# Four quarters of x are turned by VectorE's block transposes and DRAM trips instead of TensorE transposes

## The chip, the cores and the metric

The kernel runs on one core of one Trainium2 chip, in one launch. The metric is the device time of an execution in microseconds (us). Three runs of the kernel before took 2202.17, 2202.65 and 2204.27 us; their median is 2202.65 us.

## The reference

Two transformer-like blocks on a sequence of 256 tokens of width 2048, all in float32. The first block, cut to what matters here:

```python
mem_n = rms_norm(mem, norm_mem_g)
h = rms_norm(x, norm_in_g)                       # x: (1, 256, 2048)
proj = h @ w_in                                  # to qa ka va za qb kb vb zb qm zm gates
mk, mv = split(mem_n @ w_mem_kv)
...                                              # three attentions, gated, projected, merged
x = x + merged @ w_out
x = rms_norm(x, norm_final_g)
```

The second block (an RG-LRU, a retention and a gated feed-forward layer) follows on the result. The change touches only the way from x to its transposed operand of `h @ w_in`; the same numbers are to come out.

## The kernel before, in words

**Products.** Every product takes the activations as the stationary operand, with the 2048 (or more) inputs on the partitions, and streams 512 output columns of a weight matrix. To keep float32 precision each operand is split into a high part (`_hi`, fp32r) and a rest (`_lo`), and three matmuls are summed: hi*hi, hi*lo, lo*hi (L1485, L1486, L1487). A tile of 512 output columns is worked off in eight **weight chunks**; a chunk is 256 rows of the weights (512 KB) and costs 12 matmuls (two groups of 128 rows, two groups of 128 tokens, three products). Chunks are numbered through the program in this text: g0 to g31 are the four tiles of `w_mem_kv` (`tiles_memkv`), eight a tile, and g32 is the first chunk of `w_in` (`tiles_attention`), the first that needs x.

**A chunk's way.** SyncE loads it into one of four slots of `raw` (L451); ScalarE makes `w_hi` of it (L575, `split`); VectorE makes `w_lo` (L861, `split`); TensorE multiplies. ScalarE waits for the slot to be free again (`w_used`), VectorE for ScalarE (`hi_ready`), TensorE for VectorE (`lo_ready`), SyncE for VectorE. So the engines in front of TensorE can be at most four chunks ahead of it. The order on each engine is fixed: `run` walks the chunks of a tile, and after the split of chunk h of the tile come that engine's hooks for h (`act_hooks`, `dve_hooks`; `pe_hooks` on TensorE come after the matmuls of a chunk).

**x's operand.** x comes in as token rows (`x_tok`, L467). In the tiles 2 and 3 of `tiles_memkv` TensorE transposes one **quarter** (512 of the 2048 columns) at a time (`job`, L1345: 8 transposes of 128x128 into PSUM, after g18, g20, g26 and g28); ScalarE scales them into `xT_hi` (`job_hi`, L607), VectorE makes `xT_lo` (`job_lo`, L898). ScalarE also takes x's sums of squares (`squares`, L584, after its split of g15), and VectorE makes from them x's factors after its split of g17 (`x_factors`): it sends the mean to GpSimd, which takes a power (`norm_root(1)`, L497), and goes on when that is back (L880).

**The other way to turn.** The results of projections that must be transposed go by another way already, called a **trip** here. VectorE turns 32x32 blocks of `stage` into `tmp` (`turn_blocks`, L1023, `z_made`), GpSimd's queue writes `tmp` to a DRAM scratch (L513), waits until it has landed (`b_out`), and reads it back with four DMAs that put the blocks where they belong (`carry`, L518, `b_in`). ScalarE then copies out of `stage` (`use_late`, L729). GpSimd does the trips one after another, in the order of its program. In `tiles_memkv` there are two, for the two halves of mkT: trip 1 (turned after g11) and trip 2 (turned after VectorE's split of g19, `post`: L1050 and L1023).

## Time and profile before

| | us |
|---|---|
| runs (3), median | 2202.65 |
| lowest, highest | 2202.17, 2204.27 |
| profiled execution, its own time | 2204.24 |
| profiled execution, span | 2202.4 |
| TensorE busy in the span | 2185.7 (99%) |
| VectorE busy | 1308.7 (59%) |
| ScalarE busy | 1025.3 (47%) |

The span is what the trace covers of the profiled execution, from its first to its last event; 1.84 us of that execution's time lie around it. The profiled execution is 1.59 us above the median of the runs. Times inside the trace count from the start of the span.

### The profile page before, as it was taken

How to read it: one execution, taken by the hardware profiler on the slowest of the kernel's cores; microseconds unless marked ns; L12 is line 12 of the kernel's file. 1: busy time of each engine (PE TensorE's matmuls, PEld its weight loads, DVE VectorE, ACT ScalarE, POOL GpSimd, SP SyncE). 2: the span in 40 equal slices, each digit the busy share in tenths (PEclk: the TensorE clock that was granted, in tenths of full speed). 3: DMA queues.
4: the chain of work that ended last, by engine and by line, in shares of the span. 5: the costliest groups of instructions: out<-in, count | busy, mean ns of one | idle time of the engine just before them, and what ended most of it. 6: DMA issues, size and time to landing. Idle time of an engine off the chain costs nothing.

```text
span 2202.4 us, 26200 instructions
## 1 busy us (share of the span) xinstructions
PE 2185.7 (99%) x9906; PEld 1811.4 (82%) x9906; DVE 1308.7 (59%) x1646; ACT 1025.3 (47%) x1235; POOL 144.2 (7%) x242
## 2 busy tenths in 40 slices
PE   9999999999999999999999999999999999999998
PEld 7888888887888888888888888888888888888886
DVE  5655656666455645546676878665555555554454
ACT  5544444443444444444554666454444444444443
POOL 0010101011000000000111100110001000100000
PEclk9999999999999999999999999999999999999999
DMA  8775656567754657667778756586777777776664
GB/s 293 219 230 177 203 164 214 182 225 220 219 163 148 211 177 229 201 204 282 228 259 249 229 182 200 192 247 210 211 211 225 220 211 211 227 236 193 194 194 146
DMA packets 228673, 464.65 MB, mean 211 GB/s; under 512 B 16344, under 2 KB 16608, under 8 KB 227680
## 3 DMA queue, kind: packets, MB, share of 16 engines
q1 hardware_dynamic: 212128, 408.73, 59.9%
q0 software_dynamic: 15712, 53.49, 8.0%
q8 instruction: 63, 1.03, 0.2%
q10 hardware_dynamic: 736, 1.12, 0.1%
q14 instruction: 34, 0.28, 0.0%
HBM read 437.59 MB, written 25.69 MB: 210 GB/s over the span
## 4 chain that ended last, share of the span: by engine, by line
PE 90%; DVE 4%; DMA 3%; ACT 1%; issue 1%; POOL 0%; POOLq 0%; ACTq 0%; DVEq 0%
PE ps L1485 29%; PE ps L1487 29%; PE ps L1486 29%; DVE w_lo L861 1%; DMA stage<-bounce 1%; PE ps L1345 1%; ACT w_hi L575 1%; PE ps L1376 1%; PE ps L1398 1%; DMA bounce<-tmp 1%; DVE tmp L1023 1%; DVE tmp L1014 0%; DVE stage L1009 0%; DVE stage L1018 0%; DMA raw<-in_w_out 0%
## 5 line engine op out<-in xcount | busy, mean ns | idle before, releaser
L861 DVE TENSOR_TENSOR w_lo<-raw,w_hi 128x1024 fp32r<-128x1024 f32 (+1 forms) x776 | 931.5, 1211 | 766.8 <-ACT w_hi L575 764.9
L575 ACT ACTIVATE w_hi<-raw 128x1024 fp32r<-128x1024 f32 (+1 forms) x776 | 810.3, 1050 | 917.2 <-PE ps L1487 824.5
L1485 PE MATMUL ps<-w_hi,xT_hi 128*128 128x512 f32 x1088 | 430.2, 395 | 1.6 <-DVE w_lo L861 1.6
L1487 PE MATMUL ps<-w_hi,xT_lo 128*128 128x512 f32 x1088 | 424.2, 390 | 0.0
L1486 PE MATMUL ps<-w_lo,xT_hi 128*128 128x512 f32 x1088 | 423.6, 389 | 0.0
L1485 PE MATMUL ps<-w_hi,u2T_hi 128*128 128x512 f32 x704 | 274.0, 389 | 0.0
L1487 PE MATMUL ps<-w_hi,u2T_lo 128*128 128x512 f32 x704 | 273.9, 389 | 0.0
L1486 PE MATMUL ps<-w_lo,u2T_hi 128*128 128x512 f32 x704 | 273.9, 389 | 0.0
L1485 PEld LDWEIGHTS ps<-w_hi,xT_hi 128*128 128x128 f32 x1088 | 204.4, 188 | 44.1 <-DVE w_lo L861 3.3
L1487 PEld LDWEIGHTS ps<-w_hi,xT_lo 128*128 128x128 f32 x1088 | 204.2, 188 | 43.5
L1486 PEld LDWEIGHTS ps<-w_lo,xT_hi 128*128 128x128 f32 x1088 | 204.5, 188 | 40.7
L1486 PEld LDWEIGHTS ps<-w_lo,u2T_hi 128*128 128x128 f32 x704 | 132.2, 188 | 27.5
L1487 PEld LDWEIGHTS ps<-w_hi,u2T_lo 128*128 128x128 f32 x704 | 132.2, 188 | 27.3
L1485 PEld LDWEIGHTS ps<-w_hi,u2T_hi 128*128 128x128 f32 x704 | 132.2, 188 | 27.3
L1485 PE MATMUL ps<-w_hi,uT_hi 128*128 128x512 f32 x384 | 152.3, 397 | 0.0
L1487 PE MATMUL ps<-w_hi,uT_lo 128*128 128x512 f32 x384 | 149.7, 390 | 0.0
L1486 PE MATMUL ps<-w_lo,uT_hi 128*128 128x512 f32 x384 | 149.5, 389 | 0.0
L1485 PE MATMUL ps<-w_hi,ffT_hi 128*128 128x512 f32 x336 | 130.7, 389 | 0.0
L1486 PE MATMUL ps<-w_lo,ffT_hi 128*128 128x512 f32 x336 | 130.7, 389 | 0.0
L1487 PE MATMUL ps<-w_hi,ffT_lo 128*128 128x512 f32 x336 | 130.7, 389 | 0.0
L513 POOL DMA_DIRECT2D bounce<-tmp x41 | 23.9, 583 | 1360.6 <-DVE tmp L1023 1360.6
L518 POOL DMA_DIRECT2D stage<-bounce x164 | 98.8, 631 | 142.7 <-DMA bounce<-tmp 137.1
(262 smaller groups left out, 2259.3 us busy)
## 6 DMA issues: line engine op xcount, KB each, us to landing
raw<-in_w_in SPq DMA_DIRECT2D x368, 512.0 KB, 4.5
raw<-in_w_ffn_gate SPq DMA_DIRECT2D x88, 512.0 KB, 4.3
raw<-in_w_ffn_up SPq DMA_DIRECT2D x88, 512.0 KB, 4.5
raw<-in_w_ffn_down SPq DMA_DIRECT2D x88, 512.0 KB, 4.0
raw<-in_w_out SPq DMA_DIRECT2D x64, 512.0 KB, 5.1
bounce<-tmp POOLq DMA_DIRECT2D x41, 512.0 KB, 3.3
...
```

The costliest lines, as they stand in the source:

```text
L513: pool.dma_start(bounce, tmp[:, :, :].rearrange("p t n -> p (t n)")).then_inc(b_out, 16)
L518: pool.dma_start(stage[32 * m:32 * (m + 1), :, :].rearrange("p t (q x) -> p t q x", q=4), bounce.rearrange("(q a) (t m x) -> m a t q x", a ...
L575: nc.scalar.activation(w_hi[:, s, 0:per], raw[:, s, 0:per], ACT.Copy).then_inc(hi_ready, 1)
L861: nc.vector.tensor_tensor(w_lo[:, s, 0:per], raw[:, s, 0:per], w_hi[:, s, 0:per].bitcast(F32), ALU.subtract)\
L1023: ins = nc.vector.transpose(tmp[:, t], src(t).rearrange("p (c m a) -> p m c a", c=4, m=4))
L1345: ins = nc.tensor.transpose(ps[:, o:o + P], src(t, c), ident)
L1376: ins = nc.tensor.matmul(ps[:, o:o + P], qT[:, qc, t * P:(t + 1) * P], kT[:, kc, kt * P:(kt + 1) * P], start=n == 0, stop=n == len(qs) - 1)
L1398: ins = nc.tensor.matmul(ps[:, o:o + width], probsT[:, a + n * P:a + (n + 1) * P], v(kt), start=n == 0, stop=n == len(blocks) - 1)
L1485: nc.tensor.matmul(bank(2 * par + t), x_hi, w_hi[:, s, k], start=first, stop=False)
L1486: nc.tensor.matmul(bank(2 * par + t), x_hi, w_lo[:, s, k], start=False, stop=False)
L1487: ins = nc.tensor.matmul(bank(2 * par + t), x_lo, w_hi[:, s, k], start=False, stop=last)
```

## The change

TensorE's four jobs on x are gone, and with them `job_hi` and `job_lo` for x. For each quarter q of x now:

- VectorE transposes the quarter's 32x32 blocks from `x_tok` into `x_tmp[q % 2]` (`x_turn(q)`, two instructions), after its splits of g15, g19, g23 and g27;
- GpSimd's queue takes it through a DRAM scratch of its own into `x_stage[q % 2]` (`carry_x(q)`: one DMA out, a wait until it has landed, four DMAs in);
- ScalarE makes `xT_hi` from `x_stage` (`x_hi(q)`, four instructions), after its splits of g20, g24, g28 and g32;
- VectorE makes `xT_lo` (`x_lo(q)`, four instructions), after its splits of g21, g25, g29 and g33.

TensorE waits for `xT_lo`'s quarters before g32, g34, g36 and g38. The loads of x come in another order (both token halves of a quarter one after the other, the same eight DMAs), with a semaphore for each quarter.

```diff
...
         zm = at("zm", [P, NT, 1024], F32, 144)
         mv = at("mv", [P, NT, 1024], F32, 152)
         mkT = at("mkT", [P, 8, S], F32, 160)
+        x_tmp, x_stage = ([at(f"{n}{k}", [P, NT, NW], F32, kib + 4 * k) for k in range(2)] for n, kib in (("x_tmp", 168), ("x_stage", 176)))
         half_at = (120, 160)
         qaT, kaT, va, za = (
             [at(f"{n}{h}", s, F32, half_at[h] + 4 * m) for h in range(2)]
...
         ls8 = small[:, 118:126]
         lam = cols[:, V_LAM:V_LAM + 8]
         bounce = nc.dram_tensor("bounce", (P, NT * NW), F32, kind="Internal").ap()
-        turned = stage[:, :, :].rearrange("p t (q c b) -> p c (t q) b", c=QUAD, b=32)
+        x_bounce = [nc.dram_tensor(f"x_bounce{k}", (P, NT * NW), F32, kind="Internal").ap() for k in range(2)]
+        turned, *x_quarter = (m[:, :, :].rearrange("p t (q c b) -> p c (t q) b", c=QUAD, b=32) for m in (stage, *x_stage))
 
         def by_block(ap):
             return ap.rearrange("p c (u b) -> p c u b", b=32)
...
         dve_link = sem("dve_link")
         in_mem = [sem(f"in_mem{q}") for q in range(QUAD)]
         in_tables = sem("in_tables")
-        in_x = [sem("in_x0"), sem("in_x1")]
+        in_x = [sem(f"in_x{q}") for q in range(QUAD)]
         in_const, in_vec, in_res, in_g1, in_dec, in_gw, in_g2 = (
             sem(n) for n in ("in_const", "in_vec", "in_res", "in_g1", "in_dec", "in_gw", "in_g2"))
         spilled, in_h2, stored = sem("spilled"), sem("in_h2"), sem("stored")
         x_added, row_made = sem("x_added"), sem("row_made")
+        x_turned, x_out, x_hi_made, x_lo_made = (sem(n) for n in ("x_turned", "x_out", "x_hi_made", "x_lo_made"))
+        x_in = [sem(f"x_in{q}") for q in range(QUAD)]
         t0_done, t0_hi, t0_lo = (sem(n) for n in ("t0_done", "t0_hi", "t0_lo"))
         acc_done, rows_added, rows_sq, rows_mean, rows_root, rows_scaled = (
             sem(n) for n in ("acc_done", "rows_added", "rows_sq", "rows_mean", "rows_root", "rows_scaled"))
...
 
             def load_x(t, q):
                 c = slice(q * NW, (q + 1) * NW)
-                sp.dma_start(x_tok[:, t, c], x[t * P:(t + 1) * P, c]).then_inc(in_x[t], 16)
+                sp.dma_start(x_tok[:, t, c], x[t * P:(t + 1) * P, c]).then_inc(in_x[q], 16)
 
             sp.dma_start(ident, consts_d[:, C_ID:C_ID + P]).then_inc(in_const, 16)
             load_mem(0)
             first, second, *rest = tiles_memkv()
             load(first, {0: lambda: load_mem(1), 2: lambda: load_mem(2), 3: lambda: load_mem(3)})
-            load(second, {h: lambda h=h: load_x(h // QUAD, h % QUAD) for h in range(NT * QUAD)})
+            load(second, {h: lambda h=h: load_x(h % NT, h // NT) for h in range(NT * QUAD)})
             sp.dma_start(consts[:, C_ID + P:], consts_d[:, C_ID + P:]).then_inc(in_tables, 16)
             load_all(rest + tiles_attention() + tiles_merge(0))
             w.rounds(sp, NG - 1, lambda i: load_all(tiles_merge(i + 1)))
...
                         pool.dma_start(stage[32 * m:32 * (m + 1), :, :].rearrange("p t (q x) -> p t q x", q=4),
                                        bounce.rearrange("(q a) (t m x) -> m a t q x", a=32, t=NT, m=4)[m]).then_inc(b_in, 16)
 
+            def carry_x(q):
+                pool.wait_ge(x_turned, q + 1)
+                pool.dma_start(x_bounce[q % 2], x_tmp[q % 2][:, :, :].rearrange("p t n -> p (t n)")).then_inc(x_out, 16)
+                pool.wait_ge(x_out, 16 * (q + 1))
+                for m in range(4):
+                    pool.dma_start(x_stage[q % 2][32 * m:32 * (m + 1), :, :].rearrange("p t (q x) -> p t q x", q=4),
+                                   x_bounce[q % 2].rearrange("(q a) (t m x) -> m a t q x", a=32, t=NT, m=4)[m]).then_inc(x_in[q], 16)
+
             norm_root(0, R["mem"]["r"])
             carry(1, 1)
+            carry_x(0)
             norm_root(1, R["x"]["r"])
-            carry(2, 17)
+            carry(2, 2)
+            for q in range(1, QUAD):
+                carry_x(q)
+            carry(3, 17)
             pool.wait_ge(w_used, G_X + SLOTS)
             for t in range(NT):
                 pool.dma_start(x1[:, t], x[t * P:(t + 1) * P, :]).then_inc(in_res, 16)
...
             four[0]["act_hooks"] = {1: jobs(memT_hi, V_MEM, 1), 3: jobs(memT_hi, V_MEM, 2), 5: jobs(memT_hi, V_MEM, 3),
                                     6: [mem_in, lambda: squares(mem_tok, sumsq_m, lambda t: None)]}
             four[1]["act_hooks"] = {7: [lambda: act.wait_ge(b_out, 16),
-                                        lambda: squares(x_tok, sumsq_x, lambda t: act.wait_ge(in_x[t], 16 * QUAD))]}
-            for n in (2, 3):
-                four[n]["act_hooks"] = {6: jobs(xT_hi, V_IN, 2 * n - 4), 7: jobs(xT_hi, V_IN, 2 * n - 3)}
-            last = four[3]["act_hooks"].pop(7)
-            four[3]["act_hooks"][5] = [log_sigmoid_exp]
+                                        lambda: squares(x_tok, sumsq_x, lambda t: [act.wait_ge(s, 16 * NT) for s in in_x])]}
+            def x_hi(q):
+                act.wait_ge(x_in[q], 64)
+                for c in range(QUAD):
+                    kc = q * QUAD + c
+                    ins = nc.scalar.activation(xT_hi[:, kc].rearrange("p (u b) -> p u b", b=32), x_quarter[q % 2][:, c], ACT.Copy,
+                                               scale=cols[:, V_IN + kc:V_IN + kc + 1])
+                ins.then_inc(x_hi_made, 1)
+
+            four[2]["act_hooks"] = {4: [lambda: x_hi(0)]}
+            four[3]["act_hooks"] = {0: [lambda: x_hi(1)], 4: [lambda: x_hi(2)], 5: [log_sigmoid_exp]}
             act.dma_start(vec_a[:, :], vecs[0:P]).then_inc(in_vec, 16)
             act.dma_start(vec_b[0:V_END - P, :], vecs[P:V_END]).then_inc(in_vec, 16)
             act.wait_ge(pool_c, 1)
...
             four[0]["act_hooks"][0] = [second_half]
             prev = chain(four, None)
             tiles = tiles_attention()
-            tiles[0]["act_hooks"] = {1: last}
+            tiles[0]["act_hooks"] = {0: [lambda: x_hi(3)]}
             prev = chain(tiles, prev)
             prev = chain(tiles_merge(0, first=True), prev)
             w.rounds(act, NG - 1, lambda i: chain(tiles_merge(i + 1), merge_last(i)))
...
 
             four[0]["dve_hooks"] = {0: [second_half], 1: jobs(memT_hi, memT_lo, V_MEM, 1), 3: jobs(memT_hi, memT_lo, V_MEM, 2),
                                     5: jobs(memT_hi, memT_lo, V_MEM, 3), 7: [mem_factors]}
-            for n in (2, 3):
-                four[n]["dve_hooks"] = {6: jobs(xT_hi, xT_lo, V_IN, 2 * n - 4), 7: jobs(xT_hi, xT_lo, V_IN, 2 * n - 3)}
-            last = four[3]["dve_hooks"].pop(7)
-            four[2]["dve_hooks"][1] = [x_factors]
+            def x_turn(q):
+                dve.wait_ge(in_x[q], 16 * NT)
+                if q >= 2:
+                    dve.wait_ge(x_out, 16 * (q - 1))
+                for t in range(NT):
+                    ins = nc.vector.transpose(x_tmp[q % 2][:, t], x_tok[:, t, q * NW:(q + 1) * NW].rearrange("p (c m a) -> p m c a", c=4, m=4))
+                ins.then_inc(x_turned, 1)
+
+            def x_lo(q):
+                dve.wait_ge(x_hi_made, q + 1)
+                for c in range(QUAD):
+                    kc = q * QUAD + c
+                    lo, hi = (m.rearrange("p (u b) -> p u b", b=32) for m in (xT_lo[:, kc], xT_hi[:, kc].bitcast(F32)))
+                    ins = nc.vector.scalar_tensor_tensor(lo, x_quarter[q % 2][:, c], cols[:, V_IN + kc:V_IN + kc + 1], hi,
+                                                         ALU.mult, ALU.subtract)
+                ins.then_inc(x_lo_made, 1)
+
+            four[1].setdefault("dve_hooks", {})[7] = [lambda: x_turn(0)]
+            four[2]["dve_hooks"] = {1: [x_factors], 3: [lambda: x_turn(1)], 5: [lambda: x_lo(0)], 7: [lambda: x_turn(2)]}
+            four[3]["dve_hooks"] = {1: [lambda: x_lo(1)], 3: [lambda: x_turn(3)], 5: [lambda: x_lo(2)]}
             first_lo(t0_hi, range(2), t0_lo)
             prev = chain(four, None)
             log_sigmoid()
             tiles = tiles_attention()
-            tiles[0]["dve_hooks"] = {1: last}
+            tiles[0]["dve_hooks"] = {1: [lambda: x_lo(3)]}
             prev = chain(tiles, prev)
             prev = chain(tiles_merge(0, first=True), prev)
             w.rounds(dve, NG - 1, lambda i: chain(tiles_merge(i + 1), merge_last(i)))
...
             four = tiles_memkv()
             begin(four[0], mem_tok, in_mem)
             four[0]["need"][0].append(lambda: pe.wait_ge(cols_ready, 1))
-            for n in (2, 3):
-                four[n]["pe_hooks"] = {k: [lambda q=q: job(q, x_tok, in_x)] for k, q in ((2, 2 * (n - 2)), (4, 2 * (n - 2) + 1))}
             prev = chain(four, None)
             tiles = tiles_attention()
-            tiles[0]["need"] = {0: [lambda: pe.wait_ge(tx_free[0], w.n["j0"] - 1), lambda: pe.wait_ge(tx_free[1], w.n["j1"] - 1)],
-                                4: [lambda: pe.wait_ge(tx_free[0], w.n["j0"])],
-                                6: [lambda: pe.wait_ge(tx_free[1], w.n["j1"])]}
+            tiles[0]["need"] = {2 * q: [lambda q=q: pe.wait_ge(x_lo_made, q + 1)] for q in range(QUAD)}
             prev = chain(tiles, prev)
             tiles = tiles_merge(0, first=True)
             for k, units in ((3, 4), (4, 12), (5, 16)):
```

In the names below, `x_tmp_64`, `x_tmp_65` and `x_stage_66`, `x_stage_67` are the two buffers of each kind. The line numbers after the change are 4 to 34 higher.

GpSimd's queue from trip 1 of mkT on, before: `bounce` and `stage` are mkT's trips, the TENSOR_TENSOR is the power for x's factors.

```order
L497 TENSOR_TENSOR small<-small,mneg_c 128x2
L513 DMA bounce<-tmp 128x1024
L518 DMA stage<-bounce 32x8x128 x4
L497 TENSOR_TENSOR small<-small,mneg_c 128x2
L513 DMA bounce<-tmp 128x1024
L518 DMA stage<-bounce 32x8x128 x4
```

The same place after the change:

```order
L517 DMA bounce<-tmp 128x1024
L522 DMA stage<-bounce 32x8x128 x4
L527 DMA x_bounce<-x_tmp_64 128x1024
L530 DMA x_stage_66<-x_bounce 32x8x128 x4
L501 TENSOR_TENSOR small<-small,mneg_c 128x2
L517 DMA bounce<-tmp 128x1024
L522 DMA stage<-bounce 32x8x128 x4
L527 DMA x_bounce<-x_tmp_65 128x1024
L530 DMA x_stage_67<-x_bounce 32x8x128 x4
L527 DMA x_bounce<-x_tmp_64 128x1024
L530 DMA x_stage_66<-x_bounce 32x8x128 x4
```

The trip of x's quarter 0 now stands between trip 1 of mkT and the power; those of the quarters 1 to 3 stand behind trip 2 of mkT (the last of them is cut off here).

ScalarE from x's squares on, before (the first row of splits is g16 to g19, and so on):

```order
L584 ACTIVATE sq_out,small<-x_tok 128x2048 x2
L575 ACTIVATE w_hi<-raw 128x1024 x4
L729 ACTIVATE mkT<-stage 128x1024
L575 ACTIVATE w_hi<-raw 128x1024 x3
L607 ACTIVATE xT_hi<-ps,cols 128x256 x4
L575 ACTIVATE w_hi<-raw 128x1024
L607 ACTIVATE xT_hi<-ps,cols 128x256 x4
L575 ACTIVATE w_hi<-raw 128x1024 x4
```

The same place after the change:

```order
L600 ACTIVATE sq_out,small<-x_tok 128x2048 x2
L591 ACTIVATE w_hi<-raw 128x1024 x4
L745 ACTIVATE mkT<-stage 128x1024
L591 ACTIVATE w_hi<-raw 128x1024
L805 ACTIVATE xT_hi<-x_stage_66,cols 128x256 x4
L591 ACTIVATE w_hi<-raw 128x1024 x4
L805 ACTIVATE xT_hi<-x_stage_67,cols 128x256 x4
L591 ACTIVATE w_hi<-raw 128x1024 x3
```

ScalarE now makes `xT_hi` of quarter 1 between its splits of g24 and g25, out of `x_stage_67`.

VectorE from its split of g16 on, after the change (the row ahead of them is quarter 0's block transposes):

```order
L1306 STREAM_TRANSPOSE x_tmp_64<-x_tok 128x512 x2
L883 TENSOR_TENSOR w_lo<-raw,w_hi 128x1024 x2
L890 TENSOR_SCALAR small<-small 128x2
L902 TENSOR_TENSOR small<-small 128x2
...
L883 TENSOR_TENSOR w_lo<-raw,w_hi 128x1024 x2
L1072 TENSOR_SCALAR stage<-ps,small 128x512 x2
L1045 STREAM_TRANSPOSE tmp<-stage 128x512 x2
L1306 STREAM_TRANSPOSE x_tmp_65<-x_tok 128x512 x2
L883 TENSOR_TENSOR w_lo<-raw,w_hi 128x1024 x2
L1314 SCALAR_TENSOR_TENSOR xT_lo<-x_stage_66,cols,xT_hi 128x256 x4
```

Two pairs of block transposes of x are new here, one ahead of the factors' wait for GpSimd (L902) and one behind the turning of mkT's second half.

## Rows read from the trace of the kernel before

**Rows 1.** The page of the profile: busy times, and the chain that ended last.

```profile
PE 2185.7 (99%) x9906; PEld 1811.4 (82%) x9906; DVE 1308.7 (59%) x1646; ACT 1025.3 (47%) x1235; POOL 144.2 (7%) x242
...
PE 90%; DVE 4%; DMA 3%; ACT 1%; issue 1%; POOL 0%; POOLq 0%; ACTq 0%; DVEq 0%
```

**Rows 2.** The timeline of TensorE (start us, us, what): g18, first job, g24, g25.

```profile
62.17 0.39 PE L1485 MATMUL ps<-w_hi,memT_hi 128*128 128x512 f32 x1
...
64.66 0.39 PE L1487 MATMUL ps<-w_hi,memT_lo 128*128 128x512 f32 x1
64.89 1.03 PE L1345 MATMUL ps<-consts,x_tok 128*128 128x128 f32 x8
65.69 0.48 PE L1485 MATMUL ps<-w_hi,memT_hi 128*128 128x512 f32 x1
66.00 0.40 PE L1486 MATMUL ps<-w_lo,memT_hi 128*128 128x512 f32 x1
...
80.31 0.39 PE L1485 MATMUL ps<-w_hi,memT_hi 128*128 128x512 f32 x1
...
83.03 0.39 PE L1485 MATMUL ps<-w_hi,memT_hi 128*128 128x512 f32 x1
```

**Rows 3.** The instructions of line L1345 (duration min/median/max in ns), first 160 us.

```profile
L1345 PE MATMUL ps<-consts,x_tok x32: 270/272/273, 64.9 to 95.6; 128*128 128x128 f32 x32
```

**Rows 4.** The timeline of VectorE, g15 to g20; brackets give the idle time before.

```profile
49.47 1.23 DVE L861 TENSOR_TENSOR w_lo<-raw,w_hi 128x1024 fp32r<-128x1024 f32 x1 [1.95 <-ACT w_hi L575]
...
57.12 0.16 DVE L868 TENSOR_SCALAR small<-small 128x2 f32<-128x2 f32 x1
58.12 0.16 DVE L880 TENSOR_TENSOR small<-small 128x2 f32<-128x2 f32 x1 [0.84 <-POOL small L497]
...
59.60 1.22 DVE L861 TENSOR_TENSOR w_lo<-raw,w_hi 128x1024 fp32r<-128x1024 f32 x1 [0.40 <-ACT w_hi L575]
...
62.54 1.40 DVE L1050 TENSOR_SCALAR stage<-ps,small 128x512 f32<-128x512 f32 x2
63.98 1.30 DVE L1023 STREAM_TRANSPOSE tmp<-stage 128x512 f32<-128x512 f32 x2
```

**Rows 5.** The timeline of ScalarE, its split of g24.

```profile
73.74 1.08 ACT L575 ACTIVATE w_hi<-raw 128x1024 fp32r<-128x1024 f32 x1
```

**Rows 6.** The timeline of GpSimd: trips 1 and 2, the power between, a later trip.

```profile
41.21 0.75 POOL L513 DMA_DIRECT2D bounce<-tmp  x1 [8.26 <-DVE tmp L1023]
49.51 2.42 POOL L518 DMA_DIRECT2D stage<-bounce  x4 [7.56 <-DMA bounce<-tmp]
57.37 0.72 POOL L497 TENSOR_TENSOR small<-small,mneg_c 128x2 f32<-128x2 f32 x1 [5.43 <-DVE small L868]
65.58 0.62 POOL L513 DMA_DIRECT2D bounce<-tmp  x1 [7.49 <-DVE tmp L1023]
70.39 2.41 POOL L518 DMA_DIRECT2D stage<-bounce  x4 [4.19 <-DMA bounce<-tmp]
...
152.94 0.57 POOL L513 DMA_DIRECT2D bounce<-tmp  x1 [14.70 <-DVE tmp L1023]
156.46 2.41 POOL L518 DMA_DIRECT2D stage<-bounce  x4 [2.94 <-DMA bounce<-tmp]
```

**Rows 7.** The stretch 49 to 60 us: busy times, granted clock, DMA share, GB/s.

```profile
49.00:60.00 11.00, 11.00 (x50) 9.10 (x49) 5.20 (x11) 7.40 (x8) 3.14 (x5) 1.00 1.01 304
```

**Rows 8.** The line L518, 0 to 300 us: issue to landing of its 24 DMAs.

```profile
DMA to landing us min/median/max: 3.7/4.6/8.2
```

**Rows 9.** The timeline of ScalarE, stretch 1058 to 1064: four copies out of stage.

```profile
1059.81 1.69 ACT L721 ACTIVATE uT_hi<-stage,cols 128x256 fp32r<-128x256 f32 x4
```

**Rows 10.** The chain in order of time at the start (start us, us, what).

```profile
3.30 0.44 PE ps L1563
...
9.37 0.43 PE ps L1539
...
10.35 0.23 PE ps L1538
```

## Prediction

> **What bounds the kernel now.** I read the page first: TensorE is busy for 99% of the span, and the chain that ended last is 90% TensorE [rows 1]. So only two things move the end: time that TensorE no longer spends, and time that it newly stands still. VectorE (59%) and ScalarE (47%) have room on average, but they run at most four chunks ahead of TensorE, so a wait of some 10 us on either reaches it. Next I read TensorE's timeline around the jobs on x. A chunk takes 2.72 us (g24 to g25 is 83.03 - 80.31) [rows 2]. Last, the timelines of VectorE, ScalarE and GpSimd between 40 and 75 us, where the change puts its pieces. The reader should see there how small the lead is: VectorE has g18 ready at 60.82 (59.60 + 1.22) [rows 4], TensorE starts it at 62.17 [rows 2].
>
> **What is removed.** Four jobs of 8 transposes on TensorE. A single transpose is recorded as 272 ns [rows 3], but they overlap, so I take the price from the starts around a job. From the matmul at 64.66 to the second one after the job, at 66.00, are 1.34 us; without the job it would be two spacings of 0.227 (2.72 / 12), so a job costs 0.89 us [rows 2]. Four jobs: 3.55 us, all of it on the path. Two lie ahead of g25, two behind. ScalarE's and VectorE's 16 + 16 copies out of PSUM are replaced by as many out of SBUF, which cost about the same (four of ScalarE's out of stage: 1.69 us [rows 9]); that edit is nothing in itself.
>
> The Trainium skill (VectorE: DVE Perf Modes, "The three transpose paths" and "Rules for kernel authors") speaks against the change: for 128x128 it says to use TensorE where a PSUM destination will do, and puts such a transpose at 390 ns. An estimate by that page's figure would put the 16 transposes behind g25 at 6.2 us and the sum below at +1.3 instead of +5.7 us; the spacing that this trace shows is 0.11 us each, and it decides.
>
> **What is added.** Eight block transposes on VectorE (0.65 us each by the pair at 63.98 [rows 4], 5.2 us together) and four DRAM trips, which GpSimd does one after the other with the trips that it has. VectorE's share is small; the trips are not. One trip is, by GpSimd's rows [rows 6]: from the issue of the write to the issue of the first read 8.30 us (41.21 to 49.51), 4.81 (65.58 to 70.39) or 3.52 (152.94 to 156.46), as the DMAs are loaded; 2.42 us for the four reads; then the landing of the last, issued 1.8 us after the first, 3.7 to 8.2 us after its issue, median 4.6 [rows 8].
>
> *Quarter 0's trip and the power.* VectorE's two transposes stand behind g15, which ends at 50.70, in idle time before g16: free, ended at 52.0. GpSimd has just issued trip 1's reads (49.51 + 2.42). It writes quarter 0 at 52.2. The DMAs are full from 49 to 60 us (share 1.01) [rows 7], so I take 6.9 us, between 8.30 and 4.81 and nearer the trip issued in the same crowd: reads from 59.1 to 61.5. Only then comes the power for x's factors, which ran at 57.37 before; it is done at 62.3 instead of 58.1. VectorE stands at L880 (58.12 before [rows 4]) and g18's split is queued behind it. From L880 to g18's split 1.1 us are needed, so g18 is ready at 64.7: TensorE starts it 2.6 us late. g19 is ready at 65.9 (its split is 1.22 too); then mkT's second half is turned (2.7 us, as 62.54 to 65.28), ended at 68.6, and quarter 1's blocks (1.3 us), and g20's split ends at 71.1. TensorE would want g20 at 70.2: another 0.9.
>
> *Quarter 1's trip.* Now GpSimd's queue sets the time. It issues mkT's trip 2 at 68.9 (0.3 after the turn, as before), its reads start at 73.7 (+4.81) and are issued by 76.1 (+2.42). Only now does it write quarter 1; with TensorE's suppliers stalled and the DMAs lighter I take 3.9 (between 3.52 and 4.81): reads from 80.0, the last at 81.8, landed at 86.4 (+4.6).
>
> *Who waits for it.* ScalarE has split g24 at 74.8 [rows 5], perhaps a little later, and stands at `x_hi(1)`. Queued behind it are the splits of g25 and all that follow. After 86.4: 1.69 for `x_hi(1)`, 1.06 for `w_hi` of g25, 1.23 for `w_lo`, 0.1 for the handoffs: TensorE starts g25 at 90.5 instead of 83.03, 7.5 us late. This does not add to the delays of g18 and g20: those are contained in it, since g24 has long been done. The same sum of TensorE's own work, without two jobs, would have started g25 at 81.26; so it stands for about 5 us after g24 (71.1 + 5 x 2.72 = 84.7 at its end, plus a little).
>
> *The rest.* Quarters 2 and 3 go through an empty queue: written at 82.4 and about 95, landed by 92 and 105. ScalarE asks for them after g28 (93 or 94) and g32 (about 101, with four chunks of lead to lose: g33 is wanted at 112). The lead hides both. VectorE's extra work, the block transposes and the log-sigmoid pieces in that stretch fit in the 2.72 us a chunk leaves beside a 1.23 us split. If the cover is gone the next late piece would be g26, whose split stands behind `x_lo(1)` (1.7 us): it is ready at about 93.2, and wanted at 93.2. Behind g32 nothing changes, and TensorE goes through to the end; two jobs less give back 1.77 us.
>
> **Sum.** +7.5 - 1.77 = +5.7 us. On the profiled execution: 2202.4 + 1.84 + 5.7 = 2209.9. That execution lies 1.59 above the median of the runs, so for the median I forecast 2208.4.
>
> *Bounds.* Low: 4.81 for quarter 0's write, 3.52 for the others, landing 3.7: power done at 60.2, mkT turned at 66.5, quarter 1 landed at 81.8, g25 at 85.9: +1.1, or 2203.8. High: 8.30, 4.81, 4.81 and landing 8.2: turned at 70.0, landed at 92.3, g25 at 96.4: +11.6, or 2214.3. Even if the power came as early as before, GpSimd's two trips in a row keep g25 from being earlier than about 84.7, which already eats the 3.55 saved.
>
> **The rivals.** A measurement of this kernel can tell about 0.2% (4.4 us) from no change.
>
> *B, quick trips, no change to be seen.* The same mechanism with its price at the low end. It decides at one point: if quarter 1 has landed before about 85.1 us, the net loss is under 4.4. For it: nearly empty trips take 3.52 and land in 3.7 to 4.6. Against it: the DMA share in this stretch is high, and the first trip of mkT took 8.30. Time: between +1.1 and +4.4, middle 2205.4.
>
> *C, the stall also costs TensorE its clock.* At the start of the trace, where its first instruction comes at 3.30 us, a matmul of 512 columns at 9.37 takes 0.43 us in the chain and one at 10.35 0.23 [rows 10]; that is the lower level of its clock (1.2 GHz) against the higher (2.4). The granted clock reads 1.00 everywhere in the profile, so that view says neither yes nor no. If it falls back in the 5 us at g25, up to 6.5 us (as from 3.30 to 9.80 at the start) run at half speed, 3.2 us lost: +8.9, 2211.6. The Trainium skill (TensorE: Matmul & The Clock Gate, "The HAM clock gate") says that a long enough idle stretch puts the clock down and that it depends on where the stretch falls; no row here shows it after the start. Late landings give about the same time, and go with this case.
>
> *D, the change does its full good.* All trips hidden: -3.55 us, 2199.1. It asks that quarter 1 has landed by about 77, when mkT's trip alone takes until 72 before quarter 1 is written at all. It is the only way to a faster kernel, and even then by under 0.2%.
>
> **How the numbers follow.** Forecast 0.50 (net between +4.4 and +8), B 0.31, C 0.15, D 0.04. Slower by over 0.2%: forecast and C, 0.65. Within 0.2%: B and nearly all of D, 0.34. Faster: 0.01. The range runs from the low bound and a little below it, for half of D, to above C and short of the high bound: 2203.3 to 2213.0; cases of one sign hold most of the chance.
>
> **What would show it.** Right: TensorE has no instruction on `x_tok`; its longest wait is about 5 us on `w_lo`, between 83 and 91 us; ScalarE's longest wait there is on the DMA `x_stage<-x_bounce`, some 10 us, ended near 86; the power on GpSimd runs near 61.5 and not 57.4; every chunk after g40 starts at the same distance from the end as before. Wrong: no wait of TensorE over 2 us between 75 and 95 (B or D), a power at 57 to 58 (quarter 0's trip does not stand in its way), waits on `xT_lo` before g32 to g38, or matmuls over 0.4 us apart after a wait (C).

## The result, and the profile after

The changed kernel takes 2215.25 us, the median of 6 runs (2212.85 to 2216.62); the kernel before, 6 runs with the three of above among them, takes 2202.41 (2199.7 to 2204.27). The ratio is 1.0056 with a 95% interval of 1.0047 to 1.0066: 12.8 us slower. The direction was forecast; the size was not. It lies 6.9 us above the forecast of 2208.4 and above the range's end of 2213.0.

| | before | after |
|---|---|---|
| profiled execution, its own time | 2204.24 | 2216.62 |
| profiled execution, span | 2202.4 | 2214.5 |
| start of g18 | 62.17 | 67.53 |
| start of g25 | 83.03 | 96.21 |

The page of the profile after: busy times and shares of the chain, as [rows 1].

```profile
PE 2185.8 (99%) x9874; PEld 1810.1 (82%) x9874; DVE 1312.2 (59%) x1654; ACT 1026.4 (46%) x1235; POOL 156.5 (7%) x262
...
PE 90%; DVE 4%; DMA 3%; ACT 1%; issue 1%; POOL 0%; POOLq 0%; SPq 0%; ACTq 0%; DVEq 0%
```

TensorE is as busy as before, though 32 instructions have gone, and the rest of the page hardly differs. What tells is TensorE's timeline between 62 and 97 us (start, duration, what; the idle time before it and what ended it in brackets), as [rows 2].

```profile
67.53 0.80 PE L1523 MATMUL ps<-w_hi,memT_hi 128*128 128x512 f32 x1 [4.48 <-DVE w_lo L883]
68.13 0.63 PE L1524 MATMUL ps<-w_lo,memT_hi 128*128 128x512 f32 x1
...
96.21 0.79 PE L1523 MATMUL ps<-w_hi,memT_hi 128*128 128x512 f32 x1 [7.89 <-DVE w_lo L883]
```

Two holes (stretches in which TensorE does nothing): 4.48 us before g18 and 7.89 before g25, both ended by VectorE's `w_lo`. After each, matmuls start 0.41 to 0.6 us apart where they start 0.23 apart elsewhere. GpSimd's timeline tells why the holes are there, as [rows 6].

```profile
50.23 2.43 POOL L522 DMA_DIRECT2D stage<-bounce  x4 [7.58 <-DMA bounce<-tmp]
52.57 0.64 POOL L527 DMA_DIRECT2D x_bounce<-x_tmp  x1
62.08 2.42 POOL L530 DMA_DIRECT2D x_stage<-x_bounce  x4 [8.87 <-DMA x_bounce<-x_tmp]
64.42 0.82 POOL L501 TENSOR_TENSOR small<-small,mneg_c 128x2 f32<-128x2 f32 x1
71.57 0.62 POOL L517 DMA_DIRECT2D bounce<-tmp  x1 [6.33 <-DVE tmp L1045]
76.00 2.42 POOL L522 DMA_DIRECT2D stage<-bounce  x4 [3.81 <-DMA bounce<-tmp]
78.32 0.65 POOL L527 DMA_DIRECT2D x_bounce<-x_tmp  x1
87.58 2.42 POOL L530 DMA_DIRECT2D x_stage<-x_bounce  x4 [8.62 <-DMA x_bounce<-x_tmp]
89.89 0.65 POOL L527 DMA_DIRECT2D x_bounce<-x_tmp  x1
93.75 2.42 POOL L530 DMA_DIRECT2D x_stage<-x_bounce  x4 [3.21 <-DMA x_bounce<-x_tmp]
```

The reader should take the differences between the starts. Quarter 0's write takes 9.51 us (52.57 to 62.08), and the power for x's factors stands behind it and its reads, at 64.42 instead of 57.37. mkT's trip 2 starts at 71.57 instead of 65.58, and its write takes 4.43. Quarter 1's write then takes 9.26 (78.32 to 87.58), quarter 2's 3.86. VectorE's and ScalarE's timelines show the two waits that come of it.

```profile
65.27 0.16 DVE L902 TENSOR_TENSOR small<-small 128x2 f32<-128x2 f32 x1 [7.73 <-POOL small L501]
...
94.93 1.23 DVE L883 TENSOR_TENSOR w_lo<-raw,w_hi 128x1024 fp32r<-128x1024 f32 x1 [14.05 <-ACT w_hi L591]
```

```profile
78.21 1.06 ACT L591 ACTIVATE w_hi<-raw 128x1024 fp32r<-128x1024 f32 x1 [2.32 <-DMA raw<-in_w_mem_kv]
92.25 1.70 ACT L805 ACTIVATE xT_hi<-x_stage,cols 128x256 fp32r<-128x256 f32 x4 [12.98 <-DMA x_stage<-x_bounce]
```

VectorE stood 7.73 us for the power, ScalarE 12.98 us for quarter 1 of x, with the split of g25 queued behind it; VectorE and then TensorE followed. The stretches of 5 us around the second hole (start:end, length, busy time and count of TensorE, its weight loads, VectorE, ScalarE, GpSimd; then granted clock, DMA share, GB/s):

```profile
90.00:95.00 5.00, 0.00 (x0) 0.00 (x0) 0.07 (x1) 2.75 (x6) 1.79 (x4) 0.61 0.46 162
95.00:100.00 5.00, 3.79 (x9) 3.02 (x10) 5.00 (x8) 5.00 (x7) 1.17 (x2) 0.50 0.78 213
...
105.00:110.00 5.00, 5.00 (x23) 4.14 (x23) 3.41 (x7) 1.68 (x3) 1.97 (x4) 1.00 0.94 333
```

The granted clock reads 0.61 and 0.50 there. 0.50 is 1.2 GHz instead of 2.4, and the 0.43 us between matmuls are the same thing seen from the other side. It is back at 1.00 by 105; the matmuls are 0.23 us apart again from 101.43 on.

**The account of the trace.** g25 starts 13.18 us late (96.21 - 83.03). Its twelve matmuls last until 101.43, 5.22 us instead of 2.72: 2.5 more. The two jobs saved behind g25 give back 1.77. That makes 13.9. At the first matmul of g36 (114.77 before, 128.64 after) the two traces are 13.87 apart. Of these, 0.72 us were there already at g14, ahead of quarter 0's block transposes, which leaves 13.15 for the change. The span as a whole is 12.1 longer; the rest is given back where this one execution of the kernel before stood for 2.4 us on `w_lo` far behind (after 130 us) and the other for 0.2, and the traces of experiments 5 and 6 gain there too. It belongs to that execution, not to the change.

### The profile page after: what moved, and what is told of

Read it like the earlier page. It is cut to its first block, busy times and chain, and to the rows that moved or that the text cites. A ratio compares the mean times of both kernels' runs of the same rounds, so it can differ in the third digit from the quotient of the medians.

```text
span 2214.5 us, 26165 instructions
## 1 busy us (share of the span) xinstructions
PE 2185.8 (99%) x9874; PEld 1810.1 (82%) x9874; DVE 1312.2 (59%) x1654; ACT 1026.4 (46%) x1235; POOL 156.5 (7%) x262
## 3 DMA queue, kind: packets, MB, share of 16 engines
q8 instruction: 63, 1.03, 0.2%
## 4 chain that ended last, share of the span: by engine, by line
PE 90%; DVE 4%; DMA 3%; ACT 1%; issue 1%; POOL 0%; POOLq 0%; SPq 0%; ACTq 0%; DVEq 0%
PE ps L1523 29%; PE ps L1525 29%; PE ps L1524 29%; DVE w_lo L883 1%; ACT w_hi L591 1%; DMA x_bounce<-x_tmp 1%; PE ps L1414 1%; PE ps L1436 1%; PE ps L1383 1%; DMA bounce<-tmp 1%; DMA raw<-in_w_mem_kv 0%; DVE tmp L1045 0%; DMA raw<-in_w_out 0%; DMA raw<-in_w_in 0%; DVE tmp L1036 0%
```

## The experiments

The theory that the trace suggested: the change costs time only by **where things queue**. The power stands behind quarter 0's trip, quarter 1 behind two trips, and both are asked for too early. These rivals stood against it: the 8 extra block transposes or the added DMA traffic cost time by themselves; quarter 1's write was long because the loads that pile up in a stall burst in front of it; the low clock is a cost of its own; and the 3.5 us gain is not there at all. Twelve kernels were run, in three groups with the kernel before on the same chip (its medians 2202.47, 2203.36 and 2203.26). The last column is read from the profiled executions: by how much more than the kernel before the kernel needed from the first matmul of g14 to that of g40. It leaves out by how much the two executions differ ahead of the change and far behind it.

| | kernel | median | ratio to before [95%] | g14 to g40, us |
|---|---|---|---|---|
| | after | 2215.25 | 1.0056 [1.0047, 1.0066] | +13.15 |
| 1 | after, power first | 2210.99 | 1.0041 [1.0027, 1.0054] | +10.81 |
| 2 | after, x taken up later | 2209.41 | 1.0030 [1.0018, 1.0043] | +7.46 |
| 3 | 1 and 2 | 2206.40 | 1.0017 [1.0008, 1.0026] | +0.97 |
| 7 | 3, log-sigmoid later | 2203.45 | 1.0002 [0.9993, 1.0011] | +1.03 |
| 9 | 7, writes overlapped | 2202.36 | 0.9994 [0.9985, 1.0003] | -2.68 |
| 4 | before, jobs on x cut | 2200.06 | 0.9992 [0.9983, 1.0001] | -3.04 |
| 5 | before, trips added | 2203.63 | 1.0005 [0.9996, 1.0014] | 0.00 |
| 6 | before, turns added | 2204.02 | 1.0002 [0.9993, 1.0011] | 0.00 |
| 10 | 5, trips apart | 2204.29 | 1.0005 [0.9996, 1.0015] | +3.65 |
| 8 | after, TensorE kept busy | 2216.83 | 1.0064 [1.0050, 1.0078] | +13.01 |
| 11 | after, quarter 3 later | 2215.67 | 1.0054 [1.0041, 1.0068] | +13.85 |
| 12 | 11, TensorE kept busy | 2213.11 | 1.0044 [1.0030, 1.0058] | +9.53 |

### 1. The power ahead of quarter 0's reads

```diff
-            carry_x(0)
+            write_x(0)
             norm_root(1, R["x"]["r"])
+            read_x(0)
```

`write_x` is the first half of `carry_x`, up to the DMA out, `read_x` the wait for it and the four reads.

> The changed kernel, but GpSimd's queue writes quarter 0, takes the power for x's factors, and only then waits for the write and reads it back. Everything else is as in the changed kernel. Theory 1 (the waits standing in the queues make the loss, and TensorE's clock falls in them): the power is back near 58 us, TensorE's wait before g18 (4.5 us in the changed kernel) and the slow matmuls behind it are gone, 5 to 6 us earlier there; quarter 1's trip still ends late, so TensorE still waits some 7 us for g25 and its clock falls there: about 6 us above the kernel before, 2208. Of the 9 us that quarter 1's write took: if it was the burst of weight loads behind the first stall, it now takes about 5 us; if it was that the write stands right behind the four reads of mkT's trip on the same queue, it still takes about 9 and g25 comes no earlier than 90. Rival, theory 2 (the added traffic and VectorE's added work cost it, wherever the waits stand): no change from 2215.

Measured: 2210.99, some 4 us less than the changed kernel and 3 more than expected. Its five runs spread from 2209.60 to 2216.28, so the trace shows the mechanism better than the median does. GpSimd's timeline:

```profile
58.59 0.72 POOL L501 TENSOR_TENSOR small<-small,mneg_c 128x2 f32<-128x2 f32 x1 [6.13 <-DVE small L894]
...
73.56 0.65 POOL L527 DMA_DIRECT2D x_bounce<-x_tmp  x1
81.11 2.42 POOL L532 DMA_DIRECT2D x_stage<-x_bounce  x4 [6.90 <-DMA x_bounce<-x_tmp]
```

The power runs at 58.59, and the hole before g18 is gone; 1.35 us before g20 (69.34), 0.33 before g21 and 1.00 before g33 (116.77, behind quarter 3) are left. The second hole stays, 8.02 us:

```profile
91.92 0.80 PE L1527 MATMUL ps<-w_hi,memT_hi 128*128 128x512 f32 x1 [8.02 <-DVE w_lo L887]
```

Two things follow. The first hole comes from the power's place in the queue. And quarter 1's write still takes 7.55 us (73.56 to 81.11), though no stall came before it that could have piled up loads: the length of the writes is not explained by a burst after the hole. The profiled execution was this kernel's slowest (2216.28). Part of that lies far behind the change, where TensorE stood for 1.85 us at 1102.30 and its matmuls then came 0.43 us apart until 1106.

### 2. x's quarters taken up four chunks later

```diff
-            four[2]["act_hooks"] = {4: [lambda: x_hi(0)]}
-            four[3]["act_hooks"] = {0: [lambda: x_hi(1)], 4: [lambda: x_hi(2)], 5: [log_sigmoid_exp]}
+            four[3]["act_hooks"] = {0: [lambda: x_hi(0)], 4: [lambda: x_hi(1)], 5: [log_sigmoid_exp]}
...
-            tiles[0]["act_hooks"] = {0: [lambda: x_hi(3)]}
+            tiles[0]["act_hooks"] = {0: [lambda: x_hi(2)], 4: [lambda: x_hi(3)]}
```

and the same for `x_lo` and `x_turn` on VectorE.

> The changed kernel, but ScalarE and VectorE take up each quarter four chunks later (quarter 0 at g24 and g25, 1 at g28 and g29, 2 at g32 and g33, 3 at g36 and g37; the block transposes of quarters 2 and 3 three chunks later). Same instructions and same DMAs as in the changed kernel. Theory 1: TensorE's wait before g25 (7.9 us) and its slow matmuls (2.4 us) go, those before g18 (5.4 and 1.3) stay: about 2205. Theory 2: about 2215, since no work is taken away.

Measured: 2209.41, 6 us less than the changed kernel, and 4 more than expected. The hole at g25 is gone. Three are left: 3.56 us before g18 (the power again), 1.10 before g29 and 2.38 before g32 (109.25). After the first and the last the clock is low: matmuls come 0.43 us apart from 66.08 to 68.64 and from 110.14 to 113.1.

### 3. Both

> Both edits of the two runs before. Theory 1: no wait of TensorE that the kernel before does not have, no slow matmuls, and four jobs less: 3.5 us under the kernel before, 2199. Theory 2: the added 4 MB of traffic and 5 us of VectorE's work show: at or above the kernel before, up to 2215.

Measured: 2206.40. The expectation failed by 7 us: with both queues put right the kernel is still slower than before, by 0.8 to 2.6 parts in a thousand. So the two waits are not the whole cause. TensorE's trace shows what is left: 0.88 us before g20, 0.47 before g29 and the largest before g32:

```profile
106.11 0.47 PE L1526 MATMUL ps<-w_hi,xT_hi 128*128 128x512 f32 x1 [2.40 <-DVE w_lo L886]
```

Here the split of g32 stands behind the log-sigmoid pieces on VectorE, a chain of small operations that stood there before too. What had used up VectorE's lead is quarter 1 once more, which landed only at 91.27. ScalarE's take-up of it, and VectorE's split of g29, which is queued behind that:

```profile
91.27 1.71 ACT L809 ACTIVATE xT_hi<-x_stage,cols 128x256 fp32r<-128x256 f32 x4 [3.15 <-DMA x_stage<-x_bounce]
```

```profile
93.96 1.23 DVE L886 TENSOR_TENSOR w_lo<-raw,w_hi 128x1024 fp32r<-128x1024 f32 x1 [4.58 <-ACT w_hi L595]
```

From 93.96 to the end of the split of g32, at 106, VectorE works without a wait: it began this work without a lead, and the log-sigmoid pieces (100.15 to 104.83) then push g32 out. In the kernel before they ran from 94.58 and were hidden.

ScalarE also waits longer for weights. Its waits in the first 130 us (us in total, times, longest), in this kernel and in the kernel before:

```profile
ACT w_hi L595 <- DMA raw<-in_w_mem_kv: 27.3, 14, 4.0
```

```profile
ACT w_hi L575 <- DMA raw<-in_w_mem_kv: 15.5, 9, 2.6
```

These waits don't go with the loss: experiment 5, with the same trips, has 17.7 us of them, and experiment 9, the best of all, 30.2. Why they are longer here is not shown.

The profiled execution (2204.70) is among the four fastest of eleven, and lost only 1 us between g14 and g40 where the median lost 3.9. Its clock stayed up after the hole of 2.40 us. The mean granted clock is 0.999 in it and 0.997 or 0.998 in eight of the eleven runs, so a low clock may make up part of the difference in the others; no trace of them shows it.

### 4. What a job is worth

```diff
-                transposes(lambda t, c: src[:, t, (q * QUAD + c) * P:(q * QUAD + c + 1) * P], (4 + 2 * pair) * NW, QUAD)\
-                    .then_inc(tx_done[pair], 1)
+                if src is mem_tok:
...
+                else:
+                    o = (4 + 2 * pair) * NW
+                    ins = nc.tensor.transpose(ps[:, o:o + P], src[:, 0, q * QUAD * P:(q * QUAD + 1) * P], ident)
```

This is the kernel before with one transpose in each job on x; seven eighths of x's transposes are left out.

> The kernel before, but each of TensorE's four jobs on x does one of its eight transposes (the rest of x's operand is what stood in PSUM before, so seven eighths of the transposes are left out). It prices the jobs: by 0.89 us a job 7/8 of 3.55, 3.1 us, is gone: 2199.3. If the transposes were hidden under the matmuls around them, 2202.4; if each cost its recorded 0.27 us, 7.6 us would go.

Measured: 2200.06, ratio 0.9992 [0.9983, 1.0001], and in the trace every chunk behind the jobs 3.53 us earlier. Of these, 0.49 us were there before the first job, so 28 transposes less give 3.04 us, 0.109 each. The gain that the change was to bring is real, about 3.5 us for all 32, and a bit too small for the timing to tell.

### 5 and 6. The trips alone, the turns alone

Experiment 5 adds the four trips to the kernel before, straight from `x_tok`, and uses nothing of what they bring:

```diff
+            write_x(0)
             norm_root(1, R["x"]["r"])
-            carry(2, 17)
+            read_x(0)
+            carry(2, 2)
+            for q in range(1, QUAD):
...
+                write_x(q)
+                read_x(q)
+            carry(3, 17)
```

> The kernel before, with TensorE's jobs on x as they were, plus the four DRAM trips of x's quarters in GpSimd's queue, straight from the token rows, in the order of the run with both edits (write of quarter 0, power, read, mkT's trip 2, quarters 1 to 3). Nobody uses what they bring. So only the 4 MB of traffic are added, in the stretch 52 to 108 us, and no work on VectorE. The run with both edits lost 5.9 us more than its four jobs had given back. If the traffic did that, by making weight loads late: ScalarE's waits for weight loads in the first 130 us rise from 15.5 to 20 us or more, TensorE stands 2 to 5 us more, 2205 to 2207. If VectorE's added pieces and the order of its work did it: 2202.5, no change.

Experiment 6 adds the eight block transposes to the kernel before, and uses nothing of them:

```diff
+            four[1].setdefault("dve_hooks", {})[7] = [lambda: x_turn(0)]
+            four[2]["dve_hooks"][3] = [lambda: x_turn(1)]
+            four[2]["dve_hooks"][7].append(lambda: x_turn(2))
+            four[3]["dve_hooks"][3] = [lambda: x_turn(3)]
```

> The kernel before plus the eight block transposes of x on VectorE after g15, g19, g23 and g27, whose results nobody uses; no trips. 5.2 us of VectorE's work alone. I expect it hidden: 2202.5, within 1 us. If VectorE's lead is what fails, the wait shows before g20 (0.1 to 1 us) and before g32 (the log-sigmoid pieces take 4.5 us there).

Measured: 2203.63 and 2204.02, ratios 1.0005 and 1.0002 with 1 inside both intervals. In the traces the distance to the kernel before is the same at g14 and at g40, to 0.01 us, in both. Neither the traffic nor VectorE's work costs time by itself. ScalarE's waits for weights are 17.7 us in experiment 5, and not the 20 or more that the traffic was to cause. But the trips are slow here as well. GpSimd's timeline in experiment 5, and the stretch of quarter 1's write:

```profile
51.93 0.80 POOL L529 DMA_DIRECT2D x_bounce<-x_tok  x1
...
60.52 2.44 POOL L534 DMA_DIRECT2D x_stage<-x_bounce  x4 [2.80 <-DMA x_bounce<-x_tok]
...
72.22 0.80 POOL L529 DMA_DIRECT2D x_bounce<-x_tok  x1
82.04 2.42 POOL L534 DMA_DIRECT2D x_stage<-x_bounce  x4 [9.02 <-DMA x_bounce<-x_tok]
```

```profile
72.22:82.04 9.82, 9.82 (x45) 8.13 (x44) 5.15 (x7) 4.95 (x8) 0.80 (x3) 1.00 1.02 335
```

Quarter 0's write takes 8.59 us, quarter 1's 9.82 with the DMA share at 1.02 and no hole anywhere before it. That is as long as the 9.26 of the changed kernel. So such a write needs no stall ahead of it: it comes in a stretch in which the DMAs are full with the weights of a TensorE that runs on.

### 7. Log-sigmoid later

Experiment 3 with VectorE's log-sigmoid pieces behind the split of g54:

```diff
             prev = chain(four, None)
-            log_sigmoid()
             tiles = tiles_attention()
...
+            tiles[2]["dve_hooks"] = {6: [log_sigmoid]}
```

> The run with both edits, and VectorE's 23 small log-sigmoid pieces (4.5 us in a row) moved from behind g31 to behind g54, where VectorE has its full lead. In the run with both edits TensorE stood 2.4 to 2.8 us before g32, whose split stood behind them. If that wait comes from VectorE having no lead left when they begin: gone, 2.5 us less than there, about 2203.5. If g32 is late for its weight load, no gain.

Measured: 2203.45, as expected, 3.0 us under experiment 3, and no longer to be told from before. The wait before g32 is gone. What is left is one hole before g29 for quarter 1, which ScalarE asks for four chunks later now and still waits for:

```profile
91.43 1.71 ACT L809 ACTIVATE xT_hi<-x_stage,cols 128x256 fp32r<-128x256 f32 x4 [5.86 <-DMA x_stage<-x_bounce]
```

```profile
95.39 0.50 PE L1526 MATMUL ps<-w_hi,memT_hi 128*128 128x512 f32 x1 [2.46 <-DVE w_lo L886]
...
96.05 0.63 PE L1528 MATMUL ps<-w_hi,memT_lo 128*128 128x512 f32 x1
96.48 0.63 PE L1526 MATMUL ps<-w_hi,memT_hi 128*128 128x512 f32 x1
```

The first two matmuls after the hole are quick, and then the clock falls: the matmuls come 0.43 us apart from 96.05 to 99.0, and g29 and g30 together take 1.6 us more for it.

### 9. Quarter 1's write beside mkT's

GpSimd now issues quarter 1's write right behind that of mkT's trip 2, before it waits for either:

```diff
+            pool.dma_start(bounce, tmp[:, :, :].rearrange("p t n -> p (t n)")).then_inc(b_out, 16)
+            write_x(1)
+            pool.wait_ge(b_out, 32)
...
+            read_x(1)
```

> The run with the log-sigmoid pieces later (e7), and quarter 1's write to DRAM issued right behind the write of mkT's trip 2, before that one's wait, so that the two writes are under way together; the reads follow in the same order. There TensorE stood 2.5 us before g29, because quarter 1 landed only at 91.4. If the trips standing one after the other are what is left: quarter 1 lands 5 us or more earlier, TensorE has no wait between 60 and 130 us, 3.5 us under the kernel before, 2199 to 2200. If the two writes only share the DMAs and quarter 1 lands as late: 2203.5 as there.

```profile
67.33 0.58 POOL L542 DMA_DIRECT2D bounce<-tmp  x1 [3.19 <-DVE tmp L1056]
68.52 0.55 POOL L527 DMA_DIRECT2D x_bounce<-x_tmp  x1 [0.60 <-DVE x_tmp L1317]
...
74.28 2.52 POOL L532 DMA_DIRECT2D x_stage<-x_bounce  x4
```

Quarter 1's reads are issued at 74.28, when in the changed kernel its write had not begun (78.32). ScalarE no longer waits for it, and of TensorE's holes one of 0.53 us before g20 is left. Measured: 2202.36, 1.1 us under experiment 7 and 0.9 under the kernel before, with an interval of 0.9985 to 1.0003; expected were 2199 to 2200. In the trace it is 2.68 us quicker than the kernel before from g14 to g40. It is the best form of the change that was found, and a timing can tell it neither from no change nor from the full gain. ScalarE's waits for weights have risen to 30.2 us in the first 130; the lead that the hooks leave covers them.

### 10. Why are the writes long?

Experiment 5 with each write held back until the reads before it have landed:

```diff
-                if q >= 2:
-                    pool.wait_ge(x_in[q - 2], 64)
+                if q < 2:
+                    pool.wait_ge(b_in, 64 * (q + 1))
+                else:
+                    pool.wait_ge(x_in[q - 1], 64)
```

> The run with the trips alone (e5), but each write of a quarter waits until the four reads before it have landed. There the writes took 8.6, 9.8, 7.4 and 5.9 us, a trip of mkT before the change 4.8 or 3.5 where it stands alone. If a write is slow because it stands behind its own queue's reads: 4 to 5 us each now. If it is slow because the DMAs are full: as there, where the DMA share in the stretch is still 0.9 and more. The time is of no interest here: no change, 2203.

```profile
60.51 0.68 POOL L531 DMA_DIRECT2D x_bounce<-x_tok  x1 [8.76 <-DMA stage<-bounce]
...
82.83 0.67 POOL L531 DMA_DIRECT2D x_bounce<-x_tok  x1 [5.04 <-DMA stage<-bounce]
...
96.93 0.68 POOL L531 DMA_DIRECT2D x_bounce<-x_tok  x1 [4.95 <-DMA x_stage<-x_bounce]
```

Measured: 2204.29, no change by the timing. The stretches of the first three writes (granted clock, DMA share and GB/s at the end), and below them two of the changed kernel, where both writes stand directly behind reads:

```profile
60.51:64.95 4.44, 2.65 (x12) 1.91 (x11) 2.95 (x8) 4.09 (x5) 1.42 (x2) 1.00 0.46 183
82.83:89.56 6.73, 6.73 (x32) 5.56 (x31) 3.42 (x3) 4.10 (x5) 0.67 (x1) 1.00 0.90 310
96.93:100.51 3.58, 3.58 (x22) 3.05 (x21) 2.94 (x12) 1.32 (x2) 0.68 (x2) 1.00 0.95 333
```

```profile
78.32:87.58 9.26, 9.26 (x43) 7.66 (x42) 2.56 (x4) 0.95 (x1) 0.64 (x2) 1.00 0.94 297
89.89:93.75 3.86, 0.00 (x0) 0.00 (x0) 0.00 (x0) 1.50 (x4) 0.66 (x2) 0.66 0.63 221
```

The four writes take 4.44, 6.73, 3.58 and 6.43 us, where experiment 5 had 8.6, 9.8, 7.4 and 5.9. Three are shorter by 3 to 4 us, but they also ran at another time, the first at a share of 0.46. And in the changed kernel a write directly behind reads took only 3.86, at a share of 0.63, while TensorE stood.

The writes of all traces up to 115 us give a pattern (without quarter 1's of experiment 9, which ran beside another). At DMA shares of 0.87 and more, a write issued less than 1 us behind reads of its queue took 7.13 us (experiment 10, at 68.26) to 10.41 (experiment 2, quarter 1), and one without reads so close 3.58 to 6.73. At shares under 0.7 even those directly behind reads took only 3.68 to 6.08. The exception is mkT's trip 1: GpSimd had issued nothing for 7 us or more ahead of its write, and it took 7.75 to 8.61 at shares of 1.02 to 1.04. So a write was long where the DMAs were full and reads of its own queue were under way, but trip 1 shows that full DMAs can be enough; how much each of the two adds these runs don't settle.

The holding back has its price: the power for x's factors comes at 61.12, and TensorE stands for 1.79 us before g18, with a low clock after it.

### 8, 11 and 12. The clock

Experiment 8 is the changed kernel with spare transposes of the identity on TensorE, whose result nobody uses, to keep it at work in the two holes:

```diff
+            four[2]["need"] = {2: [lambda: warm(36)]}
+            four[3]["need"] = {1: [lambda: warm(66)]}
```

> The changed kernel, with spare transposes of the identity on TensorE in its two waits: 36 before g18 (4.0 us at 0.11 each, the wait is 4.9 us) and 66 before g25 (7.3 us of 8.0), their results unused. They do nothing but keep TensorE at work. If its clock falls in the waits and costs 1.3 us behind the first and 2.4 behind the second: matmuls 0.227 us apart right after both waits, and 3.7 us less than the changed kernel, 2211.5. If the slow matmuls have another cause: no change, 2215.

```profile
62.05 4.09 PE L1567 MATMUL ps<-consts 128*128 128x128 f32 x36
66.06 0.50 PE L1523 MATMUL ps<-w_hi,memT_hi 128*128 128x512 f32 x1
66.39 0.39 PE L1524 MATMUL ps<-w_lo,memT_hi 128*128 128x512 f32 x1
```

The clock stays up in both holes: behind the spare transposes the matmuls come 0.23 to 0.34 us apart at once. But the time is 2216.83, nothing won. What was won at g25 was lost eight chunks later, where TensorE stood for g33 and the clock fell after all. ScalarE and TensorE:

```profile
113.77 1.71 ACT L805 ACTIVATE xT_hi<-x_stage,cols 128x256 fp32r<-128x256 f32 x4 [6.37 <-DMA x_stage<-x_bounce]
```

```profile
117.73 0.50 PE L1523 MATMUL ps<-w_hi,xT_hi 128*128 128x512 f32 x1 [2.38 <-DVE w_lo L883]
...
119.08 0.63 PE L1525 MATMUL ps<-w_hi,xT_lo 128*128 128x512 f32 x1
119.51 0.63 PE L1523 MATMUL ps<-w_hi,xT_hi 128*128 128x512 f32 x1
```

ScalarE stood for quarter 3, whose trip is the last of x's in the queue. The slow clock had cost its 2.5 us while that trip was under way anyway. And the new hole brought a low clock of its own, 0.43 us between matmuls from 119.08 to 122.4: of the 4.3 us lost between g32 and g40, 2.55 are the hole and 1.75 the slow matmuls. To tell this apart, experiment 11 takes quarter 3 up at g36 and g37 in the changed kernel, and 12 adds the spare transposes to that:

```diff
-            tiles[0]["act_hooks"] = {0: [lambda: x_hi(3)]}
+            tiles[0]["act_hooks"] = {4: [lambda: x_hi(3)]}
```

> The changed kernel, but ScalarE takes up quarter 3 at g36 and VectorE at g37, four chunks later. In the changed kernel g33's split ended 0.4 us before TensorE wanted it, held up by ScalarE's wait for quarter 3. I expect no change from the changed kernel, 2215: that wait was just hidden.

> The run before with the spare transposes of e8 in TensorE's two waits. In e8 the clock stayed up, but TensorE then stood 2.4 us before g33 and nothing was gained. If that is because quarter 3's wait was the next one behind and took the clock's place: now the gain shows, 3 to 3.7 us under the run before, 2211.5 to 2212. If the fall of the clock costs nothing for another reason: no difference between the two runs.

Measured: 2215.67 and 2213.11. Experiment 11 alone changes nothing; with the spare transposes the median falls by 2.6, a little less than the 3 to 3.7 expected (five runs each, 2213.56 to 2216.56 against 2210.14 to 2213.77), and the cost from g14 to g40 from 13.85 to 9.53. At g25, where TensorE stands 8.13 us in 11, it is busy with spare work in 12 until 0.49 us before, and its first matmul there is at once a quick one:

```profile
93.73 0.50 PE L1523 MATMUL ps<-w_hi,memT_hi 128*128 128x512 f32 x1 [0.49 <-DVE w_lo L883]
```

Of the 4.3 us between the two traces, 2.4 are g25's twelve matmuls at full speed (2.88 us in place of 5.29); most of the rest is that quarter 1's trip ended earlier in this execution (its write took 8.76 us in place of 9.71), so that g25 began earlier. So the low clock costs some 2.5 us (2.6 by the medians) when nothing else is late next, and close to nothing when quarter 3 is.

## Why the prediction was right or wrong

- **TensorE is the bound, and only holes and saved time count**: right. Experiments 5 and 6 add four trips, or eight block transposes, where nobody on TensorE's way waits for them, and change nothing. The one addition is that matmuls behind a hole can be slow.
- **A job is worth 0.89 us, four 3.55**: right. Experiment 4 takes 3.04 us off between g14 and g40 with one transpose left of eight in each job, where 7/8 of 3.55 are 3.11; the spare transposes of experiment 8, 36 in 4.09 us, show the same 0.11 each. The recorded duration of one (272 ns, [rows 3]) is not the price in a stream. The 390 ns of the Trainium skill (VectorE: DVE Perf Modes, "The three transpose paths") stand there for bf16 and are far from either number that this float32 case shows.
- **Copies out of `x_stage` cost 1.69 for four**: right, 1.70.
- **Quarter 0's write, taken as 6.9 us**: wrong in size, 9.51, and above the high bound of 8.30. It made the power late by 7.1 us in place of 4.2, and g18 by 5.4 in place of 2.6 (0.7 of both is that this execution was already later by so much at the first turn of mkT, near 40 us). Experiment 1 shows the mechanism: with the power ahead of the reads the hole is gone. This does move g25: 2.6 of its lateness below come from here.
- **Quarter 1's write, taken as 3.9**: this is the step that failed. It took 9.26. The argument was that with the suppliers stalled the DMAs would be lighter, and the bounds were drawn from 3.52 to 4.81, although the same rows showed 8.30 [rows 6] and a share of 1.01 [rows 7]. The DMAs were not light between the two holes: the share there was 0.94, for TensorE, ScalarE and SyncE had gone on after the first hole. Experiment 5 gives 9.82 for the same write without a hole, and experiment 2 10.41.
- **Landing of quarter 1, 4.6 us after the last issue**: less, 2.9 (issued at about 89.4, landed by 92.25).
- **g25 at 90.5**: 96.21. The terms: mkT's second half turned at 71.3 instead of 68.6 (+2.7, of it 2.6 by quarter 0's write), trip 2's write 4.43 for 4.81 (-0.4), quarter 1's write +5.4, landing -1.7, handoffs -0.1: +5.9 for the +5.7 seen.
- **Where TensorE stands and for whom**: right. The longest wait is on `w_lo` before g25, ScalarE's longest on `x_stage<-x_bounce`, 12.98 us, and the two jobs are given back behind g25 as said (1.81). The extra 0.9 us before g20 did not come: the slow matmuls of g18 gave VectorE that time. Where the clock stayed up there is such a wait (0.34 and 0.35 us in experiments 8 and 12).
- **Rival C, the clock, chance 0.15**: it came true beside the forecast, and not in its place. The forecast held the clock at full speed through a hole of 5 us. It fell after both, and g25's chunk took 2.5 us more, where C had 3.2. So 5.7 of the miss is g25's delay and 2.5 the clock, 8.2 together at g40. By the medians the miss is 7.1 (12.8 slower where 5.7 was forecast), and by the spans 6.4: the kernel before lost 1.8 far behind that the other did not.
- **Quarters 2 and 3 hidden by the lead**: right for the kernel as it is, by a small margin. In experiment 8 TensorE came to g32 5.3 us earlier than in the changed kernel, and quarter 3 was late at once.
- **Rival B, quick trips**: no. It asked that quarter 1 had landed by 85.1; it landed at 92.25.
- **Rival D, the full good, 2199.1**: no form of the change got there. Experiment 9 removes nearly all holes and comes to 2202.36. In its trace 2.68 us of the 3.5 to be had are there, and 0.53 more were lost before g20, which leaves 0.3 without an account.

The high bound of the sum (g25 at 96.4, 2214.3) was right by luck for g25: both writes were longer than its 8.30 and 4.81, and the landing, 2.9, much shorter than its 8.2. For the kernel it was too low because it left the clock out. The range stopped short even of that. Of the signs named, one fails for another reason: chunks behind g40 do not keep their distance from the end, since the one execution of the kernel before lost 1.8 us there.

In short, the step that failed is the price of a write on the queue: 3.9 us for quarter 1's, which took 9.26, and 6.9 for quarter 0's, which took 9.51, with the clock, held at full speed, 2.5 us on top.

What stays open: how much of a write's length comes from the reads in its own queue and how much from the loads beside it; why quarter 0's write varies from 8.1 to 9.6 us between the changed kernel and experiments 2, 3 and 5, at the same place; and why ScalarE waits longer for weights in experiments 3, 7 and 9.
